# Norm roots taken per token column and spread by TensorE, with ones products in its waits, in a diffusion trunk layer

## What is computed

```python
def rmsnorm(x, g):
    x32 = x.astype(jnp.float32)
    y = x32 * lax.rsqrt(jnp.mean(x32 * x32, axis=-1, keepdims=True) + EPS)
    return (y * g.astype(jnp.float32)).astype(x.dtype)

def adaln_in(x, g, shift, scale):
    return rmsnorm(x, g) * (1 + scale) + shift

    h = adaln_in(x, g[0], sh(0), sh(1))
    x = x + 0.5 * sh(2) * rmsnorm(swiglu(h, p['w_gate'][0], p['w_up'][0], p['w_down'][0]), g[1])
    h = adaln_in(x, g[2], sh(3), sh(4))
    mix, new_ml, new_ssm = hybrid_mixer(h, p, ml_state, ssm_state, n_seg)
    x = x + sh(5) * rmsnorm(mix, g[3])
    h = adaln_in(x, g[4], sh(6), sh(7))
    x = x + 0.5 * sh(8) * rmsnorm(swiglu(h, p['w_gate'][1], p['w_up'][1], p['w_down'][1]), g[5])
```

## Time and profile before

| | us |
|---|---|
| median of 3 runs | 3206.73 (3204.51 to 3207.51) |
| the profiled execution | 3204.82 |
| its span, first to last instruction | 3202.9 |
| PE busy (matmul) | 3078.1 (96%) |
| POOL busy | 1837.7 (57%) |
| DVE busy | 1366.0 (43%) |
| ACT busy | 983.1 (31%) |
| mean granted clock | 0.977 |

### The profile page before, as it was taken

How to read it: one execution, slowest core, us unless ns; L and a number is a source line. 1 busy time by engine, 2 the same in 40 slices (tenths; PEclk the granted TensorE clock), 3 DMA queues, 4 the chain that set the end, 5 groups by cost and what they waited for, 6 DMA issues and landing times.

```text
span 3202.9 us, 50063 instructions
## 1 busy us (share of the span) xinstructions
PE 3078.1 (96%) x18189; PEld 2957.6 (92%) x18189; DVE 1366.0 (43%) x3074; ACT 983.1 (31%) x1227; POOL 1837.7 (57%) x911
## 2 busy tenths in 40 slices
PE   6799999999999999799999999799999999999996
PEld 2499999999999999699999999699999999999996
DVE  0336665566556665585753353413343111110015
ACT  2232222222222223434432233432222222223222
POOL 2366556655566555446865445566555665666663
PEclk7799999999999999899999999899999999999998
DMA  9967666665656565345444545145554544434441
GB/s 335 296 209 225 196 196 196 223 199 190 210 196 225 196 196 177 124 133 161 139 135 119 124 110 165 60 127 183 170 177 138 164 125 126 129 124 125 127 127 40
DMA packets 537316, 530.13 MB, mean 166 GB/s; under 512 B 25115, under 2 KB 534531, under 8 KB 536579
## 3 DMA queue, kind: packets, MB, share of 16 engines
q1 hardware_dynamic: 505376, 507.57, 50.2%
q10 hardware_dynamic: 31843, 21.25, 2.4%
HBM read 517.02 MB, written 9.64 MB: 164 GB/s over the span
## 4 chain that ended last, share of the span: by engine, by line
POOL 39%; issue 28%; PE 26%; DVE 4%; DMA 2%; ACT 2%; POOLq 1%; ACTq 0%; DVEq 0%
POOL w_lo L2157 36%; PE banks L671 7%; PE banks L673 7%; PE banks L672 7%; POOL hid_lo L2177 1%; PE banks L731 1%; DMA AM<-in_w_in_dram 1%; DMA w_raw<-in_w_ada_dram 1%; DVE HB L1875 1%; PE banks L697 1%; DVE banks L1500 0%; PE banks L955 0%; PE banks L1040 0%; PE banks L1060 0%; ACT AM L1155 0%
## 5 line engine op out<-in xcount | busy, mean ns | idle before, releaser
L2157 POOL TENSOR_TENSOR w_lo<-w_raw,w_hi 128x1024 fp32r<-128x1024 f32 x668 | 1597.9, 2398 | 1096.9 <-ACT w_hi L1136 1096.7
L671 PE MATMUL banks<-xn_hi,w_hi 128*128 128x384 f32 x3936 | 1342.7, 341 | 29.2 <-DVE xn_lo L1517 18.4
L673 PE MATMUL banks<-xn_hi,w_lo 128*128 128x384 f32 x3936 | 1321.7, 336 | 0.0
L672 PE MATMUL banks<-xn_lo,w_hi 128*128 128x384 f32 x3936 | 1321.5, 336 | 0.0
L1136 ACT ACTIVATE w_hi<-w_raw 128x1024 fp32r<-128x1024 f32 x668 | 705.5, 1059 | 1521.1 <-PE banks L673 907.1
L671 PEld LDWEIGHTS banks<-xn_hi,w_hi 128*128 128x128 f32 x3936 | 743.9, 189 | 51.2 <-issue 37.1
L672 PEld LDWEIGHTS banks<-xn_lo,w_hi 128*128 128x128 f32 x3936 | 743.9, 189 | 3.6 <-issue 2.9
L673 PEld LDWEIGHTS banks<-xn_hi,w_lo 128*128 128x128 f32 x3936 | 743.3, 189 | 0.0
L1586 DVE SCALAR_TENSOR_TENSOR banks<-w_raw,cT,banks 128x256 f32<-128x256 f32 x1372 | 550.6, 481 | 0.3
L671 PE MATMUL banks<-hid_hi,w_hi 128*128 128x384 f32 x1408 | 474.0, 337 | 6.6 <-POOL hid_lo L2177 6.6
L673 PE MATMUL banks<-hid_hi,w_lo 128*128 128x384 f32 x1408 | 471.1, 335 | 0.0
(11 more groups left out here) (235 smaller groups left out, 1353.2 us busy)
## 6 DMA issues: line engine op xcount, KB each, us to landing
w_raw<-in_w_ada_dram SPq DMA_DIRECT2D x288, 512.0 KB, 5.1
w_raw<-in_ffn_w_gate_dram SPq DMA_DIRECT2D x176, 512.0 KB, 3.8
w_raw<-in_ffn_w_up_dram SPq DMA_DIRECT2D x176, 512.0 KB, 3.7
w_raw<-in_ffn_w_down_dram SPq DMA_DIRECT2D x176, 512.0 KB, 3.6
w_raw<-in_w_in_dram SPq DMA_DIRECT2D x104, 512.0 KB, 3.7
w_raw<-in_w_out_dram SPq DMA_DIRECT2D x32, 512.0 KB, 3.6
HB<-row_wait ACTq DMA_DIRECT2D x12, 512.0 KB, 5.0
x_wait<-xT ACTq DMA_DIRECT2D x1, 3072.0 KB, 9.6
```

The costliest lines, as they stand in the source:

```text
L671: pe.matmul(out, wh, hi, start=start, stop=False)
L672: pe.matmul(out, wh, lo, start=False, stop=False)
L673: return pe.matmul(out, w_lo[:, w, off:off + P], hi, start=False, stop=stop)
L2157: pool.tensor_tensor(w_lo[:, slot(p), :], w_raw[:, p % NR, :], w_hi[:, slot(p), :].bitcast(F32), ALU.subtract).then_inc(w_lo_ready, 1)
```

## The change

The square's tile becomes the stationary operand. For each of three chunks of 128 tokens PE loads the chunk of squares and multiplies it by one column of ones (`token_sums`), so the sums lie as 128 tokens x 3 columns. Root and reciprocal are taken on 3 columns (`tok_std`). DVE multiplies them into three identity blocks (`diag`, 128 x 384, in `std`'s place), and PE multiplies a matrix of ones by it (`root_rows`), which puts the reciprocal of each token on all partitions of `ROOT_BANK`, as before. DVE waits for that product.

`stay_awake(n)` multiplies ones by ones, 128 columns, into bank 1, n times. It stands ahead of the wait for `diag` (4, not for x0), behind the spreading product of the y roots (6) and behind that of x1 and x2 (18). ACT takes a Sqrt of one column ahead of each FFN's last eight pieces.

```diff
--- before.py
+++ after.py
@@ -340,6 +340,7 @@
         dbc = sb("dbc", [P, P])
         small = sb("small", [P, 32])
         stats = sb("stats", [P, NCH, 6])
+        tok_std = sb("tok_std", [P, 2 * NCH + 2])
         AM = sb("AM", [P, 43 * 256])
         AX = xT[:, :, :].rearrange("p k t -> p (k t)")
         PS = ctx.enter_context(nc.psum_tensor("banks", [P, 8, 512], F32))
@@ -356,7 +357,7 @@
 
 
         sq = am(16, 2 * TOK).rearrange("p (s t) -> p s t", s=2)
-        std = am(19, TOK)
+        diag = am(19, TOK).rearrange("p (c t) -> p c t", c=NCH)
         xt = am(20.5, 4 * TOK).rearrange("p (s t) -> p s t", s=4)
 
         sg = am(27, 2 * TOK).rearrange("p (s t) -> p s t", s=2)
@@ -438,6 +439,7 @@
         sq_added_pool = sem("sq_added_pool")
 
         sq_ready, sq_added, ss_mm, std_ready, xt_done = sem("sq_ready"), sem("sq_added"), sem("ss_mm"), sem("std_ready"), sem("xt_done")
+        diag_ready, root_spread = sem("diag_ready"), sem("root_spread")
         hn_ready, xn_hi_ready, xn_lo_even, xn_lo_odd = sem("hn_ready"), sem("xn_hi_ready"), sem("xn_lo_even"), sem("xn_lo_odd")
         silu_ready, hid_ready = sem("silu_ready"), sem("hid_ready")
         hid_hi_ready, hid_lo_ready = sem("hid_hi_ready"), sem("hid_lo_ready")
@@ -721,6 +723,29 @@
                                          start=True, stop=True)
                     last.then_inc(ada_cols, 1)
 
+                def token_sums(name, squares, start, stop):
+
+                    for c in range(NCH):
+                        last = pe.matmul(sum_bank(name)[:, c:c + 1], squares[:, P * c:P * c + P], ones[:, 0:1], start=start and c == 0,
+                                         stop=stop and c == NCH - 1)
+                    last.then_inc(ss_mm, 1)
+
+                def stay_awake(n):
+
+                    for _ in range(n):
+                        pe.matmul(psum[1][:, 0:P], ones[:, :], ones[:, :], start=True, stop=True)
+
+                def root_rows(name):
+
+                    if name != "x0":
+                        stay_awake(4)
+                    pe.wait_ge(diag_ready, SQ_ORDER.index(name) + 1)
+                    pe.matmul(ROOT_BANK[:, 0:TOK], ones[:, :], diag[:, :, :].rearrange("p c t -> p (c t)"), start=True, stop=True).then_inc(root_spread, 1)
+                    if name[0] == "y":
+                        stay_awake(6)
+                    elif name != "x0":
+                        stay_awake(18)
+
                 def square_sum(name, k):
 
                     base, count = SQ[name]
@@ -728,8 +753,7 @@
                     if k == 0 and base:
 
                         pe.wait_ge(std_ready, SQ_ORDER.index(name))
-                    pe.matmul(sum_bank(name)[:, 0:TOK], ones[:, :], sq[:, (base + k) % 2, :], start=(k == 0),
-                              stop=(k == KT - 1)).then_inc(ss_mm, 1)
+                    token_sums(name, sq[:, (base + k) % 2, :], k == 0, k == KT - 1)
 
                 def added_sum(name):
 
@@ -739,9 +763,10 @@
                     if base:
 
                         pe.wait_ge(std_ready, SQ_ORDER.index(name))
-                    pe.matmul(sum_bank(name)[:, 0:TOK], ones[:, :], sq_acc, start=True, stop=(last == KT)).then_inc(ss_mm, 1)
+                    token_sums(name, sq_acc, True, last == KT)
                     for k in range(last, KT):
                         square_sum(name, k)
+                    root_rows(name)
 
 
                 pe.wait_ge(const_ready, 1)
@@ -849,6 +874,7 @@
                 ffn(0)
                 for k in range(KT):
                     square_sum("x1", k)
+                root_rows("x1")
 
 
                 def conv_transposes(n):
@@ -1104,6 +1130,7 @@
                 added_sum("y2")
                 for k in range(KT):
                     square_sum("x2", k)
+                root_rows("x2")
                 ffn(1)
 
                 for kk in range(KT // 4):
@@ -1145,7 +1172,7 @@
                 def root(name, width):
 
                     act.wait_ge(ss_mm, SUM_AT[name])
-                    act.activation(std[:, :], sum_bank(name)[:, 0:TOK], ACT.Sqrt, bias=eps[:, 0:1], scale=1.0 / width).then_inc(std_ready, 1)
+                    act.activation(tok_std[:, 0:NCH], sum_bank(name)[:, 0:NCH], ACT.Sqrt, bias=eps[:, 0:1], scale=1.0 / width).then_inc(std_ready, 1)
 
                 def hi_of(stage, tiles=range(KT)):
 
@@ -1193,6 +1220,7 @@
                                 step(part, it0, i)
                     name = "y3" if n else "y1"
                     added = KT * (FFN_IT * (n + 1) - 1) + (KT if n else 0)
+                    act.activation(tok_std[:, 2 * NCH:2 * NCH + 1], eps[:, 0:1], ACT.Sqrt)
                     for j in range(DOWN):
                         split(tail_of(n) + j)
                         for k in (2 * j, 2 * j + 1):
@@ -1497,7 +1525,10 @@
                 def inverse_root(name):
 
                     dve.wait_ge(std_ready, SQ_ORDER.index(name) + 1)
-                    link(dve.reciprocal(ROOT_BANK[:, 0:TOK], std[:, :]))
+                    link(dve.reciprocal(tok_std[:, NCH:2 * NCH], tok_std[:, 0:NCH]))
+                    dve.tensor_tensor(diag[:, :, :], idn[:, :].unsqueeze(1).broadcast_to((P, NCH, P)),
+                                      tok_std[:, NCH:2 * NCH].unsqueeze(2).broadcast_to((P, NCH, P)), ALU.mult).then_inc(diag_ready, 1)
+                    dve.wait_ge(root_spread, SQ_ORDER.index(name) + 1)
 
                 def scaled(stage, k):
```

## The result

The changed kernel took 3212.81 us, median of 12 runs (3210.95 to 3215.25), against 3205.88 us of the kernel before (12 runs, 3202.49 to 3207.51). The ratio is 1.0023, with a 95% interval of 1.0015 to 1.0032. The forecast was 3210.9 us, in a range from 3194.0 to 3216.5. The profiled execution took 3212.67 us; its span is 3210.9, 8.0 us more than before. By the medians the change costs 6.9 us.

The account below looks back on a forecast made before the run. TensorE, busy 96% of the span, bounds the kernel. x0 -0.9, y roots -2.3, x sums +8.2, x roots +0.2 less 0.3, x1 products -1.1, x2 +0.4 give +4.2 on 3206.73: 3210.9 us, range 3194 to 3216.5.

Parts of the forecast that it names:

- The sums per square: All norm sums: PE's time per square stays as before, 0.65 us at full clock and 1.28 at half clock.
- The clock on them: Both x sums: streaming one column lets the clock fall to half and nothing raises it; forecast's chance 0.63.
- When it falls, in x: x1 and x2 sums: fall 4.8 us after first scaling N, three squares done, end N + 21.6; 4.1 us lost each.
- The y sums: Sums of y1, y2, y3: the clock falls in one of three; the three y roots together change by -2.3 us.
- Rival B: Clock already falls in every y sum, x sums start cold and end at N + 23.1: +11.9, 3218.6 us; chance 0.14.
- Rival A: Clock stays up in the sums, as no idle gap is longer: -10.8 us, 3196.4 us; chance 0.23.
- x roots: Roots of x1 and x2 at half clock: 3.4 us against 3.32, no gain but +0.1 each.
- x1 products: First gate products after x1 start warm, giving back 2.6 us, of which 1.1 counts before POOL's w_lo is late.
- x2: Products after x2: nothing gained, PE waits 5.7 us for w_lo; half-clock stretch grows, 0 to +1.7, taken +0.4.
- x0: Start stage, sum to first scaling: shorter sums and root gain 0.9 us (0.3 to 1.3).
- The table load: Sqrt table load hoisted from the roots of y1 and y3: worth 0.3 us, twice, with no drain counted.

Follow-up runs that it names:

- sums_128: The changed kernel with the sums' products streaming 128 columns of ones instead of one: 3196.02 us, ratio 0.9969 to the kernel before.
- wide_x_only: The changed kernel with 128 streamed columns in the sums of x0, x1 and x2, one column in the y sums: 3200.07 us, ratio 0.9982 to before.
- no_dummies: The changed kernel without the ones products in PE's waits: 3215.96 us, ratio 1.0029 to the kernel before.
- wide_no_dummies: The changed kernel with 128 streamed columns in the sums and without ones products in PE's waits: 3200.94 us, ratio 0.9985 to before.
- wide_spread_clear: The changed kernel with 128-column sums and POOL's clearing of y cut into four parts, each behind a w_lo: 3189.23 us, ratio 0.9947 to before.
- wide_late_table: The changed kernel with 128-column sums and the Sqrt table load back at the roots y1 and y3: 3196.52 us, ratio 0.997 to before.
- ones_between: The changed kernel with two ones products behind each square of x1 and x2 but the last: median 3222.10 us, ratio 1.0065 to before.

## Why the prediction was right, and where its terms were off

There is no gain, for the reason given: the sums let the clock fall. The sign and the mechanism are as forecast, and the time lies 1.9 us over the forecast. That flatters it by 0.8 us: the forecast stood on a median of 3206.73 for the kernel before, and twelve runs have 3205.88. The change itself is +6.9 us by the medians and +8.0 by the profiled executions, against +4.2. By its own steps, in the profiled executions:

- **The sums per square.** Nothing changes per square at full clock and 1.28 us at half clock: right (squares 1.28 apart). **The clock on them**, from the burst of the earlier trace rows: right in both x stages, and sums_128 against the changed kernel shows the cause. The evidence was thinner than I took it for, so that it came out right is in part luck. The mixer has twelve such bursts. In the trace of the kernel before the clock fell behind the first alone; behind the one at 1527.48, which also follows a pause, it held, and in the changed kernel it held behind the first. Windows of a burst and of what follows, two lines of before and two of after:

```profile
1527.45:1529.50 2.05, 1.99 (x17) 2.02 (x18) 2.05 (x1) 0.00 (x0) 2.05 (x1) 1.00 0.00 0
1529.58:1532.90 3.32, 3.32 (x18) 2.86 (x17) 3.32 (x8) 2.01 (x2) 1.11 (x2) 1.00 0.65 181
```

```profile
1489.09:1491.14 2.05, 1.99 (x17) 2.02 (x18) 2.05 (x1) 0.00 (x0) 2.05 (x1) 1.00 0.72 226
1491.22:1494.54 3.32, 3.32 (x21) 3.32 (x20) 2.72 (x8) 1.80 (x2) 0.62 (x2) 1.00 0.57 159
```

- **When it falls, in x.** I took N + 4.8 and three squares; it was N + 3.9 and two. With the prediction's own formula, 3.93 + 14 x 1.28 + 0.2 = 22.05, the measured end. The term was mis-sized by 0.45 at each x stage (0.9 of the 3.8 us).
- **The y sums: the step that failed.** I had the clock fall in one of three. It fell at all three: 4.0 us after the last product at y1 (1277.75 to 1281.76), and 3.7 and 2.8 us after it at y2 and y3. The roots then take 3.1 to 3.3 us instead of 2.3, and -2.3 became -0.5: 1.8 of the 3.8 us. The step looked only at the 3.85 us of the sums. At y1 the clock fell behind them (they end at 1281.49), at y2 with their end, and the roots were cold all the same, because the spreading product comes 5.35 us after the last product (1277.75 to 1283.10). Of the three distances to the fall that I had measured, 2.3 and 4.6 us are shorter than this and 5.3 is as long, so they spoke for a cold root at two or three of three, not at one. The four dummies ahead of the spread did not hold the clock. wide_x_only prices the whole effect in y: 4 us.
- **Rival B** had this mechanism. Its condition, a fall less than 3.7 us after the last product, was met clearly only at y3; for cold roots 5.35 us is what counts. Its price for x was wrong in this kernel, since the six ones products bring the clock up again before the x sums (1.00 from 1285.2 to 1288.6). Its N + 23.1 appears where they are missing, in no_dummies. Its sum also leaves out the -0.9 of x0; with it the price is 3217.7.
- **Rival A** was wrong for the change as it stands. Its price was 3196.4 for a clock that stays up, and sums_128, where it does, took 3196.02. Its terms hold near enough (the x sums gain 1.2 each where it has 1.4, the x roots 1.1 where it has 1.0), but that the totals agree to 0.4 us is partly chance: the spans differ by 8.3 us, where it has 10.3. The page "TensorE: Matmul & The Clock Gate" of the Trainium skill (Why this matters for your kernels) asks that PE have no long idle gap between bursts. In the x1 sums PE was busy for 18.11 of 18.12 us and the clock was 0.50 all along; sums_128, with the same loads and waits, held 1.00. So avoiding idle gaps did not suffice here; that the clock falls behind one too, wide_no_dummies shows.
- **x roots.** No gain: right (3.23 against 3.31), with the dummies delaying the spread as worked out.
- **x1 products**, -1.1 with POOL's w_lo next late: right. PE waits 1.29 us for it at 1329.95. The first product after x1 is 3.47 us later than before, the one that waits 2.28: a gain of 1.19. The table has -0.64, because 0.55 is lost later in the mixer, where the stretches at half clock lie elsewhere (1488.9 before, 1530.9 after).
- **x2**, nothing gained: right; the wait was put at 5.7 and measured 5.67. The half-clock stretch behind it grew from 3.41 to 6.8 us, so the term is +0.83, inside its bounds of 0 to 1.7. wide_spread_clear confirms who was late.
- **x0**, -0.9: the root gained 1.23 (5.17 to 3.94 from sum to scaling), and the sum itself came 1.37 us sooner (76.05 against 77.42). The first FFN's products start 2.62 us sooner (121.00 against 123.63), and 2.05 us of it are still there at 1214. Then 1.5 us is lost at 1241, where the stretch at half clock is 6.8 us long instead of 3.4. So the measured -0.58 is not the price of this term.
- **The table load.** 0.3 at each of two roots: right, 0.28 each. The page "ScalarE: Activation LUTs" of the Trainium skill (What ACT_TABLE_LOAD costs) adds a drain to each switch of the table, by estimate some 2.8 us in all; wide_late_table, where the Sqrt starts 0.02 us behind the load, shows none of it.

## What to carry to other kernels

A busy row in the profile does not keep TensorE's clock up: read the granted clock beside what the products stream, and where weight loads set the pace, widen the moving operand: here the columns ran beside the loads at next to no cost (0.2 us in the y1 sums), and the time fell by 16.8 us. Ones products earned their time here only where they ended right before real work, and a faster stage is worth only what the next late engine leaves: look for a long instruction of another engine there, such as the clearing of 5.23 us, and cut it up.

## What the runs showed that I had not expected

- The clock can fall under a PE that is busy all the time: 1.4 us into sums of one column, 4.0 with 32 columns, 7.1 with 64, not with 128 (x1 stage, all after the same six ones products; at x2 1.2, 4.2 and 1.9, so that the moment is not fixed by the columns alone).
- One program can have several times: ones_between has three groups, 13 and 16 us apart, in twelve runs. That its filler, which takes twice the time at half clock, makes the difference is inferred and not shown.
- Clock stretches move between executions without any edit near them: the one at 1241 us, behind a wait for `hid_lo`, is 3.4 us long in the traces of before and sums_128, 6.8 in those of the changed kernel and wide_late_table. Runs of the kernel before spread over 5 us, and a total from one profiled execution is to be read with that in mind.
